# Differential attention: no VectorE operation reads two tensors from SBUF; the Newton step, the last products and the weight split on GpSimd

## The reference, cut to what matters

```
def _diff_attention(q, k, v, lam, lambda_init, g_subln):     # 4 heads, each with two maps m of width 32
    sc = einsum('bqhmd,bkhmd->bhmqk', qb, k) * scale
    allowed = key_chunk[None, :] <= q_chunk[:, None]         # chunks of 64 rows
    p = softmax(where(allowed, sc, -inf), axis=-1)
    a = p[:, :, 0] - lam * p[:, :, 1]
    o = einsum('bhqk,bkhe->bqhe', a, v)                      # e = 64
    return _rmsnorm(o, g_subln) * (1.0 - lambda_init)        # mean of squares over 64, eps 1e-6
```

## Time and profile before

| what | value |
|---|---|
| median of 3 runs | 2095.94 us (2090.75 to 2101.38) |
| the profiled execution | 2089.51 us, its span 2087.7 us |
| PE, DVE, ACT, POOL busy | 1888.6, 1356.2, 1084.5, 557.0 us |
| mean granted TensorE clock | 0.937 of 2.4 GHz |
| differential attention | about 1476 to 1887 us of the span |
| first and last start of L1514, once a step | 1488.6 and 1865.1 us |

### The profile page before, as it was taken

How to read it: one execution, slowest core, us unless ns; L and a number is a source line. 1 busy time by engine, 2 the same in 40 slices (tenths; PEclk the granted TensorE clock), 3 DMA queues, 4 the chain that set the end, 5 groups by cost and what they waited for, 6 DMA issues and landing times.

```text
span 2087.7 us, 34239 instructions
## 1 busy us (share of the span) xinstructions
PE 1888.6 (90%) x11552; PEld 1589.7 (76%) x11552; DVE 1356.2 (65%) x2805; ACT 1084.5 (52%) x2406; POOL 557.0 (27%) x438
## 2 busy tenths in 40 slices
PE   6999997999999999999999689998789888888998
PEld 6999997777777787877777587776566666667886
DVE  7606886677676767676777624444578888864544
ACT  6321211657575666666666524333578878772221
POOL 0000000344444444444444300102144444440000
PEclk9999999999999999999999769999689999999999
DMA  6322122001000101000101112424503031024542
GB/s 217 101 69 66 65 79 96 6 6 26 5 26 5 26 5 26 5 26 5 26 6 25 46 61 65 143 80 131 128 14 81 22 75 40 6 86 167 190 142 81
DMA packets 121867, 129.29 MB, mean 62 GB/s; under 512 B 81936, under 2 KB 94992, under 8 KB 120464
## 3 DMA queue, kind: packets, MB, share of 16 engines
q1 hardware_dynamic: 121744, 127.86, 21.0%
HBM read 85.89 MB, written 41.94 MB: 61 GB/s over the span
## 4 chain that ended last, share of the span: by engine, by line
PE 69%; DVE 17%; issue 7%; ACT 4%; POOL 2%; DMA 1%; DVEq 0%; SPq 0%; POOLq 0%; ACTq 0%
PE ps L662 8%; PE ps L648 5%; PE ps L616 5%; PE ps L617 5%; PE ps L618 5%; PE ps L603 4%; PE ps L605 4%; PE ps L604 4%; DVE small L1503 4%; PE ps L847 3%; PE ps L896 3%; PE ps L898 3%; PE ps L897 3%; DVE ring L1363 2%; PE ps L636 2%
## 5 line engine op out<-in xcount | busy, mean ns | idle before, releaser
L1643 POOL TENSOR_TENSOR ring_r<-ring,sp_hi 128x512 fp32r<-128x512 f32 (+1 forms) x320 | 358.6, 1121 | 819.4 <-DVE sp_hi L1366 819.4
L662 PEld LDWEIGHTS ps<-v,ring 128*128 128x128 f32 x2176 | 298.9, 200 | 55.1 <-DVE acc L1383 22.7
L662 PE MATMUL ps<-v,ring 128*128 128x65 f32 x2176 | 298.2, 279 | 16.4 <-DVE acc L1383 10.2
L1009 ACT ACTIVATE ring<-ps 128x512 f32<-128x512 f32 (+1 forms) x320 | 170.3, 532 | 222.5 <-PE ps L637 164.7
L1669 POOL TENSOR_TENSOR p<-p 128x1024 f32<-128x1024 f32 (+4 forms) x96 | 170.5, 1787 | 249.8 <-ACT p L1156 249.8
L1363 DVE SCALAR_TENSOR_TENSOR ring<-ring,ps 128x512 f32<-128x512 f32 (+1 forms) x320 | 191.7, 599 | 34.8 <-ACT ring L1014 32.8
L603 PE MATMUL ps<-w_hl,ht_hi 128*128 128x256 f32 x768 | 212.9, 277 | 0.7 <-DVE w_hl L1244 0.6
L605 PE MATMUL ps<-w_hl,ht_lo 128*128 128x256 f32 x768 | 212.7, 277 | 0.0
L604 PE MATMUL ps<-w_hl,ht_hi 128*128 128x256 f32 x768 | 212.7, 277 | 0.0
L616 PE MATMUL ps<-ht_hi,w_hl 128*128 128x512 f32 x448 | 200.4, 447 | 13.3 <-DVE ring L1351 7.0
L1021 ACT ACTIVATE ring<-ps 128x512 f32<-128x512 f32 (+1 forms) x320 | 170.2, 532 | 58.8 <-PE ps L648 58.1
(11 more groups left out here) (185 smaller groups left out, 4004.4 us busy)
## 6 DMA issues: line engine op xcount, KB each, us to landing
w_raw<-in_w_narrow SPq DMA_DIRECT2D x18, 512.0 KB, 3.9
xb<-in_x SPq DMA_DIRECT2D x16, 512.0 KB, 3.9
gate_scr<-ring SPq DMA_DIRECT2D x64, 128.0 KB, 1.8
qk_scr<-w_hl SPq DMA_DIRECT2D x32, 256.0 KB, 3.4
gb<-gate_scr SPq DMA_DIRECT2D x16, 512.0 KB, 3.7
yb<-y_scr SPq DMA_DIRECT2D x16, 512.0 KB, 4.6
xr<-in_x SPq DMA_DIRECT2D x16, 512.0 KB, 4.3
out_y<-ob SPq DMA_DIRECT2D x16, 512.0 KB, 2.9
```

Of the source, the lines that this page charges most:

```text
L662: mm = pe.matmul(ps[:, 4 + i % 2, j * (HD + 1):(j + 1) * (HD + 1)], ring[:, 4 + i % 2, j * P:(j + 1) * P], v1[:, kb, :], start=True, stop= ...
L1643: nc.gpsimd.tensor_tensor(ring_r[:, i % 4, j0 * P:], ring[:, i % 4, j0 * P:], sp_hi[:, i % 4, j0 * P:].bitcast(F32), ALU.subtract).then_in ...
```

## The change

- VectorE's operations with two SBUF tensors become reductions over adjacent columns: L1507 and L1514 are now tensor_reduce; for this the partial minima and sums are laid out side by side.
- kappa is made by two tensor_scalar of one column with two per-partition scalars, in place of one scalar_tensor_tensor of two columns, with minus lambda, so that GpSimd adds instead of subtracting.
- The values are multiplied by the reciprocals as they leave PSUM (df_rows), so L1552, L1555 and L1566 go.
- The Newton step and the last two products move to GpSimd, as df_norm(b), behind the difference of step 2b+5 in its queue; L1595 moves there too, behind difference and norm of its step.
- VectorE's first minimum of a step waits for df_a in place of df_p2s, and the variance of block b waits until the Newton step of block b-1 is done.

```
-                    nc.vector.tensor_tensor(df_stat(s, 4 + m), df_stat(s, m), df_stat(s, 2 + m), ALU.min).then_inc(df_mn, 1)
+                    nc.vector.tensor_reduce(df_stat(s, 4 + m), df_stat(s, 2 * m, 2), AXX, ALU.min).then_inc(df_mn, 1)
...
-                nc.vector.tensor_tensor(df_stat(s, 12, 2), df_stat(s, 8, 2), df_stat(s, 10, 2), ALU.add).then_inc(df_st, 1)
+                nc.vector.tensor_reduce(df_stat(s, 12, 2), df_stat(s, 8, 4).rearrange("p (m a) -> p m a", m=2), AXX, ALU.add).then_inc(df_st, 1)
...
-                nc.vector.scalar_tensor_tensor(out=df_stat(s, 18, 2), in0=df_stat(s, 16, 2), scalar=lam, in1=d[:, :, 0],
-                                               op0=ALU.mult, op1=ALU.mult).then_inc(df_kap, 1)
+                for r in range(2):
+                    nc.vector.tensor_scalar(df_stat(s, 18 + r), df_stat(s, 16 + r), d[:, r, 0:1], minus_lam, ALU.mult, ALU.mult
+                                            ).then_inc(df_kap, 1)
...
-                    dve.wait_ge(df_sq, b - 1)
-                nc.vector.tensor_copy(osb[:, b % 2], ps[:, 6, 0:4 * HD].rearrange("p (j d) -> p j d", j=4)).then_inc(df_ob, 1)
+                    dve.wait_ge(df_r, b - 1)
+                dve.wait_ge(df_st, 3 * (2 * b + 2))
+                nc.vector.tensor_tensor(osb[:, b % 2], ps[:, 6, 0:4 * HD].rearrange("p (j d) -> p j d", j=4),
+                                        df_rc(b).unsqueeze(2).broadcast_to((P, 4, HD)), ALU.mult).then_inc(df_ob, 1)
...
                 nc.vector.tensor_reduce(ss, osq[:], AXX, ALU.add).then_inc(df_ss, 1)
-                dve.wait_ge(df_st, 3 * (2 * b + 2))
-                nc.vector.tensor_tensor(r2, df_rc(b), df_rc(b), ALU.mult).then_inc(df_g, 1)
                 dve.wait_ge(df_ss, b + 1)
-                dve.wait_ge(df_g, 2 * b + 1)
-                nc.vector.tensor_tensor(ss, ss, r2, ALU.mult).then_inc(df_g, 1)
-                dve.wait_ge(df_g, 2 * b + 2)
+                if b:
+                    dve.wait_ge(df_nr, 4 * b)
                 nc.vector.tensor_scalar(var, ss, 1.0 / HD, EPS, ALU.mult, ALU.add).then_inc(df_var, 1)
...
+            def df_norm(b):
+                var, y0, tmp, r = df_tmp(4, 4), df_tmp(12, 4), df_tmp(16, 4), df_tmp(20, 4)
+                a = acc[:, b % 2]
+                pool.wait_ge(df_y0, b + 1)
+                pool.wait_ge(df_var, b + 1)
...
+                nc.gpsimd.tensor_tensor(tmp, y0, y0, ALU.mult).then_inc(df_nr, 1)
...
+                nc.gpsimd.tensor_tensor(tmp, tmp, var, ALU.mult).then_inc(df_nr, 1)
...
+                nc.gpsimd.tensor_scalar(tmp, tmp, -0.5, 1.5, ALU.mult, ALU.add).then_inc(df_nr, 1)
...
+                nc.gpsimd.tensor_tensor(r, tmp, y0, ALU.mult).then_inc(df_nr, 1)
...
+                nc.gpsimd.tensor_tensor(a, osb[:, b % 2], r.unsqueeze(2).broadcast_to((P, 4, HD)), ALU.mult).then_inc(df_r, 1)
...
+                nc.gpsimd.tensor_tensor(a, a, gsub_b.unsqueeze(1).broadcast_to((P, 4, HD)), ALU.mult).then_inc(df_yok, 1)
+
+            for s in range(N_SL + 6):
+                if s < N_SL:
+                    df_difference(s)
+                if s >= 5 and s % 2:
+                    df_norm((s - 5) // 2) if s < N_SL + 5 else None
+                if s in WO_SLOT:
+                    k = WO_SLOT[s]
+                    pool.wait_ge(wo_hi_ok, k + 1)
+                    pool.sem_inc(pool_go, 1)
+                    nc.gpsimd.tensor_tensor(wo_lo[:, k, :], w_raw[:, (k % 2) * D:(k % 2 + 1) * D], wo_hi[:, k, :].bitcast(F32),
+                                            ALU.subtract).then_inc(wo_lo_ok, 1)
```

More of the change, by code:

```diff
@@ L155, in build @@
         invf = small[:, 0:1]
-        lam = small[:, 1:2]
+        minus_lam = small[:, 1:2]
         qk_scale = sb("qk_scale", [P, 1], F32)
@@ L302, in build @@
             sem("df_" + n) for n in ("p2s", "a", "t", "at_a", "at_d", "o"))
-        df_oc, df_ot, df_ob, df_sq, df_ss, df_f, df_var, df_ln, df_y0, df_nr, df_r, df_g, df_yok = (
-            sem("df_" + n) for n in ("oc", "ot", "ob", "sq", "ss", "f", "var", "ln", "y0", "nr", "r", "g", "yok"))
+        df_oc, df_ot, df_ob, df_sq, df_ss, df_var, df_ln, df_y0, df_nr, df_r, df_g, df_yok = (
+            sem("df_" + n) for n in ("oc", "ot", "ob", "sq", "ss", "var", "ln", "y0", "nr", "r", "g", "yok"))
         df_pad = [sem("df_pad0"), sem("df_pad1")]
@@ L899, in out_products @@
                     mm.then_inc(o_ps, 1)
-            pe.wait_ge(df_r, N_SL // 2)
+            pe.wait_ge(df_ob, N_SL // 2)
             out_transposes(0)
@@ L1145, in df_exp @@
                 dst = (p2 if m else p1)[:, s % (3 - m), at0:at0 + keys]
-                bias, total = df_stat(s, (4 if j < 4 else 6) + m), df_stat(s, (8, 10, 8, 10, 14, 14)[j] + m)
+                bias, total = df_stat(s, (4 if j < 4 else 6) + m), df_stat(s, (8, 9, 10, 11, 14, 15)[j])
                 nc.scalar.activation(dst, df_ps(j)[:, 0:keys], ACT.Exp, bias=bias, scale=-1.0, accum_out=total).then_inc(df_e, 1)
@@ L1153, in df_weigh @@
                 first, end = ((0, KEYS), (KEYS, (big + 1) * P), ((big + 1) * P, PAIR))[part]
-                act.wait_ge(df_kap, s + 1)
+                act.wait_ge(df_kap, 2 * s + 1 + part // 2)
                 x = p2[:, s % 2, first:end]
@@ L1296, in _ @@
                     dve.wait_ge(sb_ch, 3)
-                    nc.vector.tensor_scalar(lam, small[:, 6:7], LAMBDA_INIT, None, ALU.add).then_inc(sb_ch, 1)
+                    nc.vector.tensor_scalar(minus_lam, small[:, 6:7], -1.0, -LAMBDA_INIT, ALU.mult, ALU.add).then_inc(sb_ch, 1)
                 if i < SB:
@@ L1500, in df_min @@
                 if s >= 3 and j == 0:
-                    dve.wait_ge(df_p2s, 3 * (s - 2))
+                    dve.wait_ge(df_a, 3 * (s - 2))
                 dve.wait_ge(df_z, s * UNITS + j + 1)
-                least = nc.vector.tensor_reduce(df_stat(s, (0, 2, 0, 2, 6, 6)[j] + m), df_ps(j)[:, 0:keys], AXX, ALU.min)
+                least = nc.vector.tensor_reduce(df_stat(s, (0, 1, 2, 3, 6, 7)[j]), df_ps(j)[:, 0:keys], AXX, ALU.min)
                 least.then_inc(df_mn if j >= 4 else df_b, 1)
@@ L1591, in _ @@
                     nc.vector.memset(df_qk[1][s - 2][3 * DQ:P, :, :].bitcast(F32), 0.0).then_inc(df_pad[1], 1)
[L1592 to L1596, removed]
             def out_gate(i):
@@ L1660, in _, with df_difference @@
             pool.wait_ge(df_pad[0], 2)
-            for s in range(N_SL):
-                h, big, small = df_pair(s)
+            def df_difference(s):
+                h, big, small_row = df_pair(s)
                 for k, (first, end) in enumerate(((0, KEYS), (KEYS, (big + 1) * P), ((big + 1) * P, PAIR))):
+                    a, x = p1[:, s % 3, first:end], p2[:, s % 2, first:end]
                     pool.wait_ge(df_p2s, 3 * s + k + 1)
-                    a = p1[:, s % 3, first:end]
                     pool.sem_inc(pool_go, 1)
-                    nc.gpsimd.tensor_tensor(a, a, p2[:, s % 2, first:end], ALU.subtract).then_inc(df_a, 1)
+                    nc.gpsimd.tensor_tensor(a, a, x, ALU.add).then_inc(df_a, 1)
@@ new lines, in df_norm @@
+            def df_norm(b):
[5 more added lines that the diff above has]
+                nc.gpsimd.tensor_tensor(tmp, y0, y0, ALU.mult).then_inc(df_nr, 1)
+                pool.wait_ge(df_nr, 4 * b + 1)
+                pool.sem_inc(pool_go, 1)
+                nc.gpsimd.tensor_tensor(tmp, tmp, var, ALU.mult).then_inc(df_nr, 1)
+                pool.wait_ge(df_nr, 4 * b + 2)
+                nc.gpsimd.tensor_scalar(tmp, tmp, -0.5, 1.5, ALU.mult, ALU.add).then_inc(df_nr, 1)
+                pool.wait_ge(df_nr, 4 * b + 3)
+                pool.sem_inc(pool_go, 1)
+                nc.gpsimd.tensor_tensor(r, tmp, y0, ALU.mult).then_inc(df_nr, 1)
+                pool.wait_ge(df_nr, 4 * b + 4)
+                if b >= 2:
+                    pool.wait_ge(df_yout[b % 2], 64 * (b // 2))
+                else:
+                    for u in range(4):
+                        pool.wait_ge(m_yout[u], 16 * N_MT // 4)
+                pool.sem_inc(pool_go, 1)
+                nc.gpsimd.tensor_tensor(a, osb[:, b % 2], r.unsqueeze(2).broadcast_to((P, 4, HD)), ALU.mult).then_inc(df_r, 1)
+                pool.wait_ge(df_r, b + 1)
+                pool.sem_inc(pool_go, 1)
+                nc.gpsimd.tensor_tensor(a, a, gsub_b.unsqueeze(1).broadcast_to((P, 4, HD)), ALU.mult).then_inc(df_yok, 1)
```

21 lines of the change are left out of this document (3 added, 18 removed).

## The result

The changed kernel took 2057.22 us in the median (2053.77 to 2062.9), before 2093.35 us; the ratio is 0.9836 (0.9815 to 0.9857), 34 us. The forecast was faster by 19 us, from 2096 to 2077. Their intervals are 0.002 to 0.005 to either side, so two kernels whose ratios differ by less than 0.003 can't be told apart by them.

What follows compares the result with a forecast made beforehand. The prediction took the order of waits between VectorE, TensorE and ScalarE, with GpSimd's holds, as the bound. Chain terms gave 24 us and step pairs 15; it took 19, from 2096 to 2077 us, range 2052 to 2092.

Steps and rivals of the forecast that it cites:

- The reductions' term: L1507 and L1514 as reductions escape GpSimd's holds: 9.7 us gained on the chain, and 0.5 for L1514's one hold.
- The inherited hold: The variance's tensor_scalar, standing where L1552 and L1555 stood, is held by GpSimd as they were; likeliest case, -19 us, chance 0.46.
- Rival 1: No hold is left, as the four-column tensor_scalar is held only by fills or comes before the difference: 2061 us, chance 0.26.
- the second count: Estimate by step pairs in the loop: even 10.5 us, odd 11.3, with hold 23.1 a pair against 24.1; 16 us gained.
- The hold's 1.3 us: ScalarE's root waits behind the held variance in odd steps: 18.3 us in 14 times, 1.3 each, added to the pair.
- the first count: Sum of the change's parts on the chain of waits: 24 us gained, taken as an upper bound.
- the division: Values multiplied by reciprocals as they leave PSUM, so L1552 and L1555 leave VectorE's chain: 3.3 us gained.
- the split: L1595, the low parts of w_out, moves from VectorE to GpSimd: 6.0 us gained on the chain.
- The norm: Newton step and last two products leave VectorE for GpSimd: 6.5 us gained on the chain.
- The tail: At the output stage, load_y follows norm 13 and comes later: net 1 us lost, between 4 lost and 3 gained.
- Rivals 2 and 3: kappa held in passing, 12 us lost of 19, chance 0.16; held tensor_scalars starved until GpSimd idles, 15 slower, 0.12.
- Rival 4: GpSimd's norm takes 6 us and not 3, delaying TensorE's transposes: 5 to 10 us lost; chance included in 0.16.

Runs made afterwards that it cites:

- e5_no_hold: The changed kernel with the variance's scale and epsilon on ScalarE in place of VectorE's tensor_scalar; 2040.6 us, ratio to before 0.9778.
- e6_columns: The changed kernel with the variance's four-column tensor_scalar as four of one column each; 2039.89 us, ratio to before 0.9767.
- e13_fills: The changed kernel with one-column variance operations, the first gate and y loads ahead of block 13's wait, and two fills moved to GpSimd; 2021.51 us.
- e9_tt_minimum: The changed kernel with the combined minimum (L1507) as a tensor_tensor again; 2084.63 us, ratio to before 0.9986.
- e4_divide: The kernel before with only the values divided as they leave PSUM (L1552, L1555, L1566 go); 2068.05 us, ratio 0.9882.
- e2_split: The kernel before with only the low parts of w_out (L1595) moved to GpSimd; 2086.86 us, ratio 0.9978.
- e12_norm_back_free: The changed kernel with variance scaling on ScalarE, early gate and y loads, and Newton step and last two products on VectorE again; 2034.25 us.
- e10_norm_back: The changed kernel with the Newton step and last two products on VectorE again; 2055.62 us, ratio to before 0.9833.

## Why the prediction was right and wrong

- **The mechanism was right**: a VectorE operation with two SBUF inputs is held to the end of GpSimd's tensor_tensor. The reductions run at 0.155 us, as forecast, though the reduction in the earlier trace rows reads PSUM and L1507 reads SBUF, so that row was thin ground. The reductions' term, 10.2 us, measured 13.6 alone and 9.4 in the loop.
- **The inherited hold was right**, and with it the Trainium skill's "SBUF — State Buffer", "Who interferes with whom", that a tensor_scalar between SBUF tensors can contend with GpSimd: the four-column tensor_scalar was held in all 14 odd steps, ScalarE's wait before the root was 15.2 us (forecast near 18). Rival 1 gave 36 us for "no hold is left", close to the time measured, but its reason did not happen; that agreement is luck. The time alone would have spoken for the wrong theory; L1557's row decides.
- **The prediction overlooked a nearer row.** It said that the trace of before has no tensor_scalar during a tensor_tensor of GpSimd, and went to the fills. But that trace has another operation with one SBUF input in that place, a cast of the stick-breaking attention:

```profile
375.76 1.26 DVE L1366 CAST sp_hi<-ring 128x384 fp32r<-128x384 f32 x1
...
375.52 1.28 POOL L1643 TENSOR_TENSOR ring_r<-ring,sp_hi 128x512 fp32r<-128x512 f32 x1 [375.07 <-DVE sp_hi L1366]
```

  A free one of 384 columns takes 0.36 us; this one ended 0.22 us after GpSimd's. So rival 1's "held by fills, not by tensor_tensor" could be weighed on the trace of before.
- **The step that failed is in the second count: "An odd step adds ScalarE's squares and root (0.8): 11.3."** The even step was right: 10.5 taken, the seven shortest of before took 10.45 us in the mean, and the same seven 10.30 in e5_no_hold. Without a hold an odd step is not 0.8 us longer than an even one but shorter: 9.85 us (e5_no_hold; 9.84 in e6_columns). The sums of the 13 even steps from 6 to 30 and, below, the 13 odd ones from 7 to 31 of e5_no_hold show why the two don't add:

```profile
sum 137.69, PE 133.30 PEld 98.89 DVE 99.50 ACT 127.09 POOL 86.80; mean PE 10.25 PEld 7.61 DVE 7.65 ACT 9.78 POOL 6.68
...
sum 128.43, PE 123.17 PEld 89.65 DVE 99.53 ACT 126.99 POOL 92.88; mean PE 9.47 PEld 6.90 DVE 7.66 ACT 9.77 POOL 7.14
```

  Of an even step (10.59 us) TensorE is busy for 10.25 and ScalarE for 9.78: the 10.5 us are TensorE's, and ScalarE has room in them. Of an odd step (9.88 us) ScalarE is busy for 9.77 and TensorE for 9.47, as its transposes back (L857), once in two steps, all fall in even ones. So I read each kind of step as bounded by its fullest engine, where the count put ScalarE's extra work on top of TensorE's pace; no run changed either engine's work alone. The hold's 1.3 us on top were right (1.2 measured, 21.95 against 20.73 a pair). With 9.85 in place of 11.3 the count gives 21.65 a pair and 2.45 x 15.5 = 38 us, where 35.7 were measured in the loop.
- **In the first count terms were mis-sized**: the division 3.3 us, less 1.1 for kappa (9 to 11 measured for the two), and the split 6.0 us (7 to 12). I read it as a limit of the chain: its rows give what an operation lay on the path, and not what its lateness does to the next step or to the clock. The norm was mis-sized the other way: 6.5 us forecast, 4.3 in the loop and nothing in the whole time.
- **The tail** was forecast at 1 us lost; it was 3.5, by the mechanism named (load_y behind norm 13).
- **A bound that was none**: TensorE's 322.7 us busy were to rule out a gain over 50. In e13_fills the loop took 312.9 us, 64 less than before: the 322.7 us were measured with 56.0 us at the lower clock.
- **Rivals 2 and 3 fell**: kappa's single columns were never held (0.27 us, all 64, of which 37 began during an operation of GpSimd). Their pair lasts 0.45 us where the one operation took 0.22, so 0.23 us more and not 0.1; what that cost was not tried by itself. **Rival 4 fell**: 0.20 us for four columns, 0.61 and 0.78 for the products.
- **Open**: what a hold costs on the path. It was 0.63 of its length for the variance (e5_no_hold), while the net 23 us of holds added in e9_tt_minimum cost 26.6 in the loop. There the clock was lower for longer as well; the kernels also differ in where GpSimd's work meets L1507, and no run separates the two.

## What to carry to other kernels

Look for tiny operations with a mean far above their least duration: the excess may be a hold. Here it cost on the path between 0.6 of what it lasted and all of it, so try it by removing it. When such an operation is rewritten, ask whether the next one in its place has a form that is held as well, and split it into single columns or give it to another engine if so. Estimate the pace without stalls from what each engine is busy with in each kind of step, and take the fullest one of each, and don't add one engine's extra work to another's pace. And move loads ahead of a wait when the work that they wait behind gets later.

## What the runs showed of the hardware

- Between SBUF tensors a tensor_scalar of four columns was held by GpSimd's tensor_tensor (2.09 us in the median, 0.17 free) and one of two columns by its fill (6.12 us). One of a single column was not held by its tensor_tensor, neither with immediate scalars (145 ns, 64 times in e6_columns) nor with per-partition ones (270 ns, 64 times in the kernel after).
- Of two operations that meet, the one that started first went on: in e4_divide a variance that started 0.09 us ahead of the difference took 0.17 us, and the difference its usual 2.36.
- Between two fills that follow each other at once, the held operation got in or not: L1472 took 6.11 to 6.12 us in four profiles (before, e2_split, e4_divide, e12_norm_back_free) and 2.66 to 2.68 us in the other twelve, where all ahead of it is the same.
- Save in e13_fills, the changes add no operation ahead of the loop, yet it began between 1484.9 and 1498.1 us. This does not go with L1472: with 6.11 us the loop of e12_norm_back_free began at 1486.6, with 2.67 us that of e10_norm_back at 1488.6. It goes with the clock: ahead of the loop it was at its lower level for 184 us in the profiles that began by 1485.5, 193 us in the one of before (1488.8), 205 us in those that began between 1490.0 and 1495.8, and 218 us in the one of e4_divide (1498.1). I take the 2.0 us by which the changed kernel's loop began earlier to be of this kind, and not the change's.
- GpSimd needed 0.20 us for four columns, and stood idle for about 0.18 us before most of the operations that wait for the one ahead.
